# A two-layer mixer block in one hand-ordered program: a table that shifts every kind of step by a few places, and six gates computed early and stored

## What is computed

```python
def merge_branches(ya, yb, yc, gate_logits, w_branch, w_out):
    ys = jnp.einsum('btiw,iwd->btid', jnp.stack([ya, yb, yc], axis=2), w_branch)
    gates = jax.nn.sigmoid(gate_logits.reshape(B, T, N_BRANCH, D_MODEL))
    return jnp.einsum('btd,de->bte', jnp.sum(gates * ys, axis=2), w_out)
...
    t_inv = lax.linalg.triangular_solve(eye + l_strict, ...)   # delta rule, per chunk of 64 and head
    u = jnp.einsum('bnhts,bnshv->bnthv', t_inv, v_beta)
    def step(s, inp):                                          # chunk after chunk
        v_new = u_n - jnp.einsum('bthd,bhdv->bthv', w_n, s)
        ...
```

## Time and profile before

| what | value |
|---|---|
| median of 3 runs | 2361.31 us (2359.95 to 2364.9) |
| the profiled execution, its own time | 2353.64 us |
| its span in the profile | 2351.6 us |
| PE busy | 2167.6 us, 92% of the span |
| DVE, ACT, POOL busy | 931.7, 846.4, 358.0 us |
| HBM traffic | 80 GB/s over the span |

### The profile page before, as it was taken

How to read it: one execution, slowest core, us unless ns; L and a number is a source line. 1 busy time by engine, 2 the same in 40 slices (tenths; PEclk the granted TensorE clock), 3 DMA queues, 4 the chain that set the end, 5 groups by cost and what they waited for, 6 DMA issues and landing times. The chain is left out here.

```text
span 2351.6 us, 31435 instructions
## 1 busy us (share of the span) xinstructions
PE 2167.6 (92%) x10970; PEld 1468.8 (62%) x10970; DVE 931.7 (40%) x2271; ACT 846.4 (36%) x2205; POOL 358.0 (15%) x591
## 2 busy tenths in 40 slices
PE   6999899899979989999999999988988968899998
PEld 3676576555545776555674437766575657766787
DVE  2023364656563325333331120246667653243321
ACT  2223253535443224444231112245346443244421
POOL 1000007071542000000000010000742760000000
PEclk8999899999989999999999999999999989999999
DMA  8215312211212022111222342122321312223243
GB/s 290 68 58 171 101 39 66 80 51 47 81 28 64 28 63 82 55 46 37 73 73 89 107 149 77 34 73 67 95 64 55 89 38 73 63 92 110 90 143 126
DMA packets 191419, 190.14 MB, mean 81 GB/s; under 512 B 28559, under 2 KB 185955, under 8 KB 190755
## 3 DMA queue, kind: packets, MB, share of 16 engines
q1 hardware_dynamic: 186048, 171.08, 23.5%
q0 software_dynamic: 3648, 16.72, 2.2%
q10 hardware_dynamic: 1571, 0.34, 0.1%
HBM read 178.62 MB, written 9.50 MB: 80 GB/s over the span
## 5 line engine op out<-in xcount | busy, mean ns | idle before, releaser
L1042 PE MATMUL bank<-hT,ring 128*128 128x512 f32 (+2 forms) x1856 | 727.1, 542 | 5.5 <-DMA ring<-in_w_in_dram 3.5
L1042 PEld LDWEIGHTS bank<-hT,ring 128*128 128x128 f32 (+1 forms) x1856 | 335.4, 192 | 256.1 <-issue 237.7
L1042 PE MATMUL bank<-ring,hT 128*128 128x256 f32 (+2 forms) x2112 | 458.5, 373 | 25.0 <-DMA ring<-in_w_in_dram 25.0
L1042 PE MATMUL bank<-WORK 128*128 128x128 f32 (+4 forms) x3056 | 403.7, 289 | 73.8 <-ACT WORK L1672 21.0
L1042 PEld LDWEIGHTS bank<-WORK 128*128 128x128 f32 (+3 forms) x3056 | 324.9, 172 | 188.9 <-issue 139.4
L1042 PEld LDWEIGHTS bank<-ring,hT 128*128 128x128 f32 x2112 | 385.8, 193 | 88.1 <-issue 35.6
L1042 PE MATMUL bank<-yT,ring 128*128 128x512 f32 (+1 forms) x768 | 273.4, 490 | 0.0
L1042 PEld LDWEIGHTS bank<-yT,ring 128*128 128x128 f32 x768 | 139.5, 193 | 80.2 <-issue 71.1
L1007 POOL TENSOR_TENSOR WORK<-WORK 64x31 f32<-64x31 f32 (+15 forms) x248 | 149.5, 603 | 19.4
L1977 DVE SCALAR_TENSOR_TENSOR WORK<-WORK,CW 128x512 f32<-128x512 f32 (+1 forms) x192 | 146.7, 764 | 3.0
L1005 POOL TENSOR_TENSOR WORK<-WORK 64x31 f32<-64x31 f32 (+15 forms) x248 | 139.5, 562 | 19.5
(11 more groups left out here) (202 smaller groups left out, 2071.0 us busy)
## 6 DMA issues: line engine op xcount, KB each, us to landing
ring<-in_w_in_dram SPq DMA_DIRECT2D x92, 1024.0 KB, 5.4
ring<-in_ada_w_dram SPq DMA_DIRECT2D x24, 1024.0 KB, 6.4
ring<-in_w_branch_dram SPq DMA_DIRECT2D x24, 1024.0 KB, 5.2
ring<-in_w_out_dram SPq DMA_DIRECT2D x8, 1024.0 KB, 5.0
ring<-in_mla_q_up_dram SPq DMA_DIRECT2D x8, 576.0 KB, 4.0
xs<-yT POOLq DMA_DIRECT2D x2, 2048.0 KB, 10.6
ring<-in_mla_kv_up_dram SPq DMA_DIRECT2D x8, 512.0 KB, 4.7
yT<-xs POOLq DMA_DIRECT2D x2, 2048.0 KB, 10.0
```

The source lines that it names most:

```text
L1042: return nc.tensor.matmul(o, a, b, start=start, stop=stop, skip_group_check=True)
```

## The change

A table `AHEAD` gives each kind of step a number of places. `settle` sorts the finished list by place minus that number, so a kind with 4 stands four places earlier and one with -8 eight places later; nothing is added or left out by it. Some entries: `cv` 4, `dqkv` 5, `dnq` 3, `mkv` 3, `muq` 2, `ms` 2, `dn` -1, `yT` -1, `z2` -4, `muk` -6, `abT` -7, `mo` -8, and `vdn` -2 for the DVE part of `dn`.

Of the second layer's last branch, gates 0 to 5 move out of its merge and into `gdn`, ahead of the first branch's products. A new step `gx` writes the finished gate (its Exp) into the lower half of yT, which is unused there; `ys` then reads it from there. So the last merge has gates 6 and 7, then eight `ys`.

Two orders are changed by hand: for g == 2 the convolutions of the next group (`vs`) are woven into the scan from the first on, where twelve of them had stood ahead of the scan; and `dg` stands eight places later. `gqk` of group 0 waits itself for the shifted input, and the reload of the stream also waits for DVE's last `ys`.

```diff
+def keeps(it):
+
+    return it[0] in ("gate", "ys") and it[1] == DEPTH - 1 and it[2] == 2 and it[3] < 6
...
+def settle(s):
+
+    def at(n):
+        it = s[n]
+        mark, it = (it[0], it[1:]) if it[0] == "v" else ("", it[1:-1] if it[0] == "pc" else it)
+        g = it[2] if it[0] in PHASE and PHASE[it[0]] < 2 and len(it) > 2 else 0
+        return n - AHEAD.get((mark + it[0], it[1], g), AHEAD.get(mark + it[0], 0))
+
+    return [s[n] for n in sorted(range(len(s)), key=lambda n: (at(n), n))]
...
+    def kept_gates(l):
+
+        out = []
+        for e in range(6):
+            out += pieces(("gate", l, 2, e)) + [("v", "gate", l, 2, e), ("gx", l, 2, e)]
+        return out
+
     def merge(l, br):
+        if keeps(("gate", l, br, 0)):
+            out = [i for e in range(6, 8) for i in pieces(("gate", l, br, e)) + [("v", "gate", l, br, e)]]
+            return out + [i for e in range(8) for i in pieces(("ys", l, br, e))]
...
-        return [("ab", l)] + out[:4] + [("abT", l)] + out[4:10] + [("dg", l)] + out[10:]
+        return [("ab", l)] + out[:4] + [("abT", l)] + out[4:18] + [("dg", l)] + out[18:]
...
-            out += vs[:12] + weave(steps, weave(vs[12:], mine[len(early):]))
+            n = 0 if g == 2 else 12
+            out += vs[:n] + weave(steps, weave(vs[n:], mine[len(early):]))
...
+        fill = merge(l, 0)
+        if keeps(("gate", l, 2, 0)):
+            fill = kept_gates(l) + fill
+        s += gdn(l, zs(l, 0) + yts(l, 0), fill)
...
+                elif k == "gx":
+                    gi = ("gate",) + it[1:]
+                    act.wait_ge(*done(gi, "dve"))
+                    act.wait_ge(s_spill, 16 * (l + 1))
+                    act.wait_ge(s_scaled, KT * (l + 1))
+                    ins = nc.scalar.activation(yT[:, it[3], 0:LC], E1[:, zg_index[gi] % 2, LC:T], ACT.Exp)
...
+                    if keeps(it):
+                        dve.wait_ge(*done(("gx",) + it[1:], "act"))
+                        e = yT[:, e8, 0:LC]
```

More of the change, by code:

```diff
@@ L151, in pieces @@
     return [("pc",) + it + (i,) for i in range(NPIECE[it[0]] - 1)] + [it]
+AHEAD = {('yT', 1, 0): 0, 'gw': 4, 'ga': 2, 'dnq': 3, 'yT': -1, 'cv': 4, 'ms': 2, 'mkv': 3, 'muk': -6, 'dx6': 3, 'dqkv': 5, 'd1': 1, 'muq': 2, 'dya': 3, 'vdn': -2, 'gv': 4, 'ab': 4, 'go': -3, 'dn': -1, 'mo': -8, 'vdsil2': 1, 'abT': -7, 'sq': -3, 'nx': 3, 'dy6': 3, 'dv': 1, 'dyb': 2, 'mod': -1, 'gatt': -6, 'gx': -4, 'z2': -4, 'sk': -1}
+def settle(s):
[5 more added lines that the diff above has]
+    return [s[n] for n in sorted(range(len(s)), key=lambda n: (at(n), n))]
 def schedule():
@@ L341, in schedule @@
         m = merge(l, 2)
+        lead = 5 * (8 - 6) if keeps(("gate", l, 2, 0)) else lead
         s += zs(l, 2) + weave(yts(l, 2), m[:lead]) + m[lead:]
@@ L348, in schedule @@
     s += [("xout", tt, h) for tt in tiles(DEPTH - 1) for h in range(2)]
-    return s
+    return settle(s)
 PHASE = {"lr": 0, "gqk": 0, "gv": 0, "ga": 0, "ge": 0, "gb": 0, "gatt": 0, "gw": 0, "go": 0,
@@ L626, in takes_part @@
         def takes_part(it, who):
-            return True
+            return not (it[0] == "ys" and keeps(it) and who == "act")
         def done(it, who, mark=""):
@@ L711, in hybrid_block @@
                  "dt", "sol", "dv", "dx", "dya", "dx6", "sk", "sq", "su", "sa"}
-        NODVE = {"norm", "osq", "dqkv", "pc", "dnq", "xin", "gqk", "gv", "lr", "mp", "xout", "mkT",
+        NODVE = {"gx", "norm", "osq", "dqkv", "pc", "dnq", "xin", "gqk", "gv", "lr", "mp", "xout", "mkT",
                  "dd", "sol", "dw", "dyb", "st"}
@@ L762, in claim, with input_here @@
                         pe.wait_ge(*done(b, who))
+        def input_here(pe, l, kk):
+            if kk in SHIFTED_BY_DVE[l]:
+                pe.wait_ge(s_hd, shifted(l, kk, True))
+            else:
+                pe.wait_ge(s_ha, shifted(l, kk, False))
         def rows_of(u):
@@ L1029, in _ @@
                     pool.wait_ge(*done(("ys", l, 2, 7), "pe"))
+                    pool.wait_ge(*done(("ys", l, 2, 7), "dve"))
                     pool.dma_start(yT[:, :, :], xs[l]).then_inc(s_back, 16)
@@ L1103, in _ @@
                     for kk in range(piece * n, piece * n + n):
[L1104 to L1107, removed]
+                        input_here(pe, l, kk)
                         grp = kk % NGRP_LR
@@ L1125, in _ @@
                     for kk in range(piece * n, piece * n + n):
+                        if k == "gqk" and it[2] == 0:
+                            input_here(pe, l, kk)
                         ins = mm(ps[:, a0:T], w[:, kk, :], src[:, kk, a0:T], kk == 0, kk == KT - 1)
@@ L1851, in _ @@
                     e = E1[:, zg_index[gi] % 2, q0:512]
-                    dve.wait_ge(*done(it, "act"))
+                    if keeps(it):
+                        dve.wait_ge(*done(("gx",) + it[1:], "act"))
+                        e = yT[:, e8, 0:LC]
+                    else:
+                        dve.wait_ge(*done(it, "act"))
                     m = MT[:, e8, q0:T]
```

10 lines of the change are left out of this document (6 added, 4 removed).

## The result

The changed kernel takes 2271.4 us (median of 4 runs, 2264.7 to 2273.1) against 2360.6 us for the kernel before (4 runs). The ratio is 0.9628 with a 95% interval of 0.9603 to 0.9652: 3.7% faster, some 89 us. The forecast was 2314 us, 47 us faster, with 2287 as the low end of the range. The direction was right and the size was not.

What follows compares the result with a forecast made beforehand. PE's queue was taken as the path, its work plus idle time. Terms of 50.3 us idle plus 3 clock less 6 new waits gave -47, 2306.6 profiled; 7.7 added for the median gave 2314 us, range 2287 to 2354.

Steps and rivals of the forecast that it cites:

- the 3 us for the clock: Whole kernel: removed stalls save PE some steps at the lower clock; only 3 us added, 8 at the lower end.
- the allowance for new waits: Whole kernel: 6 us charged against the gain for unnamed waits that 2400 shifted places create.
- Latent attention: Both layers' latent attention: earlier `mkv` and later `mo` remove waits, less a charge for `muk`; -6 and -5 us.
- The charge of 1.5 us per layer for `muk`: Latent attention: `muk` loses cover before `mkT`, 2.3 to 4.5 us instead of 6.4 to 8.7; 1.5 us charged per layer.
- The rival built on it: Latent attention: eight head pairs wait 4.7 us each, 38 us, 52 with clock; 2366 us; chance 0.06 shared with no change.
- Layer 1's projections: Stretch 1403 to 1563: 3 us of waits go, `ge` 2 and `dg` 1.
- The second window of layer 1: Layer 1's delta rule, second `d2` to `dx` window: 10.2 us idle, quarters come in, small inverse waits stay; -2.7 us.
- The solve as the floor: Last `d2` to `dx` windows end with POOL's solve: layer 0 floor at 728.2, layer 1 length 65 to 67 us.
- The scan copy: Group 2's scan: PE's wait for ACT's copy goes in both layers; worth -3.1 us in layer 0, nothing more in layer 1.
- The waits only move: Rival, whole kernel: removed waits reappear at the next consumer; only fill and `mq` loads gain, 21 us; 2340 us, chance 0.22.
- All of it, and more clock: Rival, whole kernel: every term in full plus more clock, since every clock dip stands behind a stall; 2294 us, chance 0.18.
- The solve gets longer by a shared port: Rival, solve windows: DVE's SBUF instructions slow POOL's steps; three windows could cost 48 us; 2374 us at 20 each; chance 0.05.

Runs made afterwards that it cites:

- The ones put into the kernel before: Kernel before, order unchanged, plus 559 products of ones by ones, results overwritten, in TensorE's 29 longest idle places: 2335.9 us, ratio 0.9913.
- the warmed kernels: Products of ones by ones added in TensorE's longest idle places: 559 in the kernel before, 2335.9 us; 351 in the changed kernel, 2259.6 us.
- the half-warmed: Products of ones by ones at half the count: 278 in the kernel before, 2332.2 us; 176 in the changed kernel, 2263.2 us.

## Why the prediction was right in kind and wrong in size

Its sum on the profiled execution was 50.3 of idle time, plus 3 of clock, less 6 for new waits: 47.3. Measured, 65.8 of idle time and 22.9 of busy time: 88.7. The 41 us that were missed fall into two nearly equal parts, so two steps of the sum failed: the 3 us for the clock (22.9 measured), and the net 44.3 us of idle time (65.8 measured).

**The clock was mis-sized, and this step failed by reasoning.** "The longest stalls stay in the solve windows, so I add only 3." The measured term is 22.9. The argument took the clock to hang on the longest stalls, which would stay. The runs show two things in its place. Waits of about 3 us in dense work can have a low clock behind them too, in some executions for 6.8 us and in others not at all; and the clock of the last solve windows themselves rose, from 0.90 and 0.84 to 0.95 and 0.91, as the 9 us waits at the scan copy went (with these waits back, in the kernel with twelve steps ahead of the scan, it is 0.88 and 0.85). By the table most of the gain came at the start, in the delta rules and in layer 1's projections, and little in latent attention. The ones put into the kernel before gave back 40 to 48 us of busy time without removing one dependence, so the debt was there to be estimated: its 145 us at the lower clock cost at most half of that.

How much of the 89 us is clock can be bounded from the medians, without the two traces: between the warmed kernels the change is worth 76 us (2335.9 to 2259.6), between the half-warmed 69, between the plain ones 89. That makes 13 to 20 us, an estimate, since the products overran their holes by different amounts in the two kernels. The Trainium skill (TensorE: Matmul & The Clock Gate, Part 1) says, of the ramp at a kernel's start, that its penalty is under 1% of a typical kernel span. Here the lower clock came back after waits all through the program, and by the 40 to 48 us it took 1.7 to 2.0% of the span. The advice of the Trainium skill there, for a kernel whose short groups of matmuls wait for transfers, to order the work so that TensorE stays warm, agrees with what the ones showed.

**The idle terms were too small by stage, and the allowance for new waits had the wrong place.** Every stage but the norm and the tail gave 2 to 4 us more than its term. The kernels with one family of shifts out say it more strongly: the attention's shifts are worth 28 us, clock included, where the forecast had 11 of idle time, and the delta rule's 36 where it had some 12. The largest: 

- Latent attention, -6 and -5 forecast, -10.2 and -8.4 measured. `mq` and `mo` were right to a few tenths (7.0 and 7.4 forecast, 6.8 and 7.5 us in the kernel without these shifts). The charge of 1.5 us per layer for `muk` was wrong: `mkT` does not wait at all. The rival built on it, 38 us of waits, is dead. `yT`'s 3 us had no term.
- Layer 1's projections, -3 forecast, -7.0 measured: `ge`'s 2.0 us went and `dg`'s wait fell from 5.6 to 3.1, where 3 had been given for both; the other 2.5 us are smaller waits.
- The second window of layer 1 was given 2.7 of its 10.2 us, "the inverse's small waits stay". They did not, and 8.9 us of idle time went. Without the kept gates this window is 74.2 us with 6.8 idle, so the gates carry most of it; by which wait was not separated. The other windows gave, in order, 0.5, 5.3 and 7.3 us of idle time where 4.5, 2.4 and 6.6 had been forecast: the first is short because of the next point.
- The 6 us "for waits that 2400 shifted places create and that I can't name" exist: 8.2 us at `d2` and 8.1 at `dya`, where 5.7 and 5.1 of them are one wait each, in layer 1. `d2`'s lies in the first window and `dya`'s in the last, which the solve bounds, so they take time that these windows have to wait out anyway.

**What held.** The solve as the floor: 66.3 us for the first layer's last window, where 66.3 had been worked out (728.2 less 661.9), and 63.5 for the second layer's, where 65 to 67 had been given. The 2.2 us came from the build: POOL's first read of the system is 7.9 us after the window's start in place of 9.9, and from there to `dx` it is 55.6 us against 55.9. The prediction had named a window under 64 us as a sign that it is wrong; this sign came, for a reason that carries 2 of the 41 us. The scan copy: worth nothing in layer 1, as forecast, and its 3.1 us in layer 0 could not be told from nothing. The new wait at `dx` of layer 0 came, at 4.2 us. In layer 1, where about 12 us were forecast, the wait stayed as it was (6.45 us before):

```profile
1889.26 0.23 PE L1084 MATMUL bank<-WORK 32*32 32x32 f32 x1 [6.22 <-DVE O L2104]
```

The window's idle time is 19.6 us (20.2 by the forecast, 65.7 less 45.5), but 5.1 of it now stand at `dya` and 2.0 at the scan copy. PE is busy for 43.9 us in it, where 45.5 were forecast. The weights came down to 11.6 us (16 forecast), `dn`'s square to 3.6 (under 8). The six gates are worth 16 us; the forecast had put 18.2 down to them and their windows together. Over the whole kernel PE's idle time was to fall to about 137 us and its busy time to stay near 2168, and they are 118.2 and 2144.7.

**The other rivals.** *The waits only move* was 2340, and is refuted: the idle time fell in seven of eight stages. *All of it, and more clock* came nearest, at 2294 and still 23 us short, and had the mechanism that the runs bear out. *The solve gets longer by a shared port*: POOL is busy for 41.08 and 40.72 us in the first two windows, against 40.64 and 40.67, and for 1.1 to 1.9 us more in the other three: 5 us in all, where the rival needed 48 in three windows. The runs do not tell what the 1.9 us are.

What stays open: what decides whether a wait of 3 us brings a low clock, since the same wait in one order did and did not. And which of the twelve shifts in the delta rule give its 36 us was not separated.

## What to carry to other kernels

Where the bounding engine is TensorE, read the time at its lower clock as a term of its own, beside idle and busy time, before costing a change: at most half of the time at 1.2 GHz can be won back (110 us less of it gave 40 to 48 here). For one wait the price can't be forecast: a wait of about 3 us in dense work came here with 0, 3.4 or 6.8 us at the lower clock, which is up to 3.4 us on top of its length. A wait in a window that another chain bounds mostly shows up again at the window's end when it is removed; so find the windows' floor first, and put movable work into them. Many small shifts, each worth a few us of wait, were worth 73 us here, and the two longest waits of all, 9 us each at the scan copy, nothing that could be told.

## What the runs showed of the hardware

Filling TensorE's waits with products that nobody reads made both kernels faster, by 21 to 26 us for the one before and by 7 to 9 for the changed one (ratios 0.9913 and 0.9891; 0.959 and 0.9599 against 0.9628; the last two are at the edge of what can be told), though up to 130 us of work were added. And identical orders do not get identical clocks: the same first stretch took 241.3 to 247.9 us in ten executions, at a mean clock of 0.950 down to 0.924, and one and the same wait, 3.0 to 3.3 us long in three executions of one order, came with 0, 3.4 and 6.8 us at the lower clock.
